# A two-layer hybrid decoder trunk on one core: 32x32 diagonal blocks inverted on VectorE, and one block level less on TensorE

## The reference, cut to what matters

```python
def chunked_gated_delta_rule(q, k, v, beta, g):
    ...
    lower = jnp.where(strict, jnp.einsum('bhncd,bhnsd->bhncs', k_beta, k) * decay, 0.0)
    eye = jnp.eye(GDN_CHUNK, dtype=lower.dtype)
    rhs = jnp.concatenate([v * beta[..., None], k_beta * jnp.exp(g)[..., None]], axis=-1)
    sol = lax.linalg.triangular_solve(lower + eye, rhs, left_side=True, lower=True, unit_diagonal=True)
    u = sol[..., :dv]
    w = sol[..., dv:]
    ...
    def step(state, xs):
        u_i, w_i, qd_i, intra_i, ks_i, cd_i = xs
        v_new = u_i - jnp.einsum('bhck,bhkv->bhcv', w_i, state)
        o_i = jnp.einsum('bhck,bhkv->bhcv', qd_i, state) + jnp.einsum('bhcs,bhsv->bhcv', intra_i, v_new)
        state = state * cd_i[..., None, None] + jnp.einsum('bhck,bhcv->bhkv', ks_i, v_new)
        return state, o_i
```

## Time and profile before

| | us |
|---|---|
| median of three executions | 2683.03 |
| the profiled execution | 2680.91 |
| its span, from the first to the last instruction | 2679.0 |
| TensorE busy (97%) | 2605.1 |
| VectorE busy (64%) | 1712.2 |
| ScalarE busy (44%) | 1176.7 |

### The profile page before, as it was taken

One profiled execution on the slowest core, in us unless ns is written; L12 is line 12 of the kernel. 1 busy time (PEld: TensorE's weight loads), 2 busy tenths in 40 slices (PEclk: granted clock), 3 DMA queues, 4 the chain that ended last, 5 costly groups with the idle time before them and its releaser, 6 DMA issues. The chain is left out here.

```text
span 2679.0 us, 35335 instructions
## 1 busy us (share of the span) xinstructions
PE 2605.1 (97%) x12554; PEld 2196.0 (82%) x12554; DVE 1712.2 (64%) x2296; ACT 1176.7 (44%) x1450; POOL 85.1 (3%) x89
## 2 busy tenths in 40 slices
PE   7998999999999999999999999999999999999997
PEld 7886888788887988788788888888788888888885
DVE  3356875787577766776666767666665645546556
ACT  1025354543555354635444444444454344453443
POOL 0000110011001000101000000000000000000000
PEclk9678999999999999999999999999999999999998
DMA  8676556764676558555688777876555665666655
GB/s 257 218 238 183 172 156 190 236 173 142 189 244 173 150 165 257 163 171 172 200 267 257 253 254 238 268 254 230 178 160 188 194 186 191 190 187 192 188 189 178
DMA packets 300997, 541.69 MB, mean 202 GB/s; under 512 B 39200, under 2 KB 44832, under 8 KB 299552
## 3 DMA queue, kind: packets, MB, share of 16 engines
q1 hardware_dynamic: 271568, 523.86, 62.8%
q10 hardware_dynamic: 29264, 15.68, 2.0%
HBM read 536.26 MB, written 3.21 MB: 201 GB/s over the span
## 5 line engine op out<-in xcount | busy, mean ns | idle before, releaser
L1038 DVE TENSOR_TENSOR w_lo<-raw,w_hi 128x1024 fp32r<-128x1024 f32 x803 | 986.0, 1228 | 700.0 <-ACT w_hi L606 658.0
L606 ACT ACTIVATE w_hi<-raw 128x1024 fp32r<-128x1024 f32 x803 | 847.5, 1060 | 1152.9 <-PE acc L1603 828.2
L1603 PE MATMUL acc<-w_hi,u_hi 128*128 128x512 f32 x2176 | 869.9, 400 | 8.3 <-DVE w_lo L1038 7.3
L1603 PE MATMUL acc<-w_hi,u_lo 128*128 128x512 f32 x2176 | 851.5, 391 | 0.0
L1603 PE MATMUL acc<-w_lo,u_hi 128*128 128x512 f32 x2176 | 850.8, 391 | 0.0
L1603 PEld LDWEIGHTS acc<-w_hi,u_hi 128*128 128x128 f32 x2176 | 411.6, 189 | 97.5 <-DVE w_lo L1038 14.5
L1603 PEld LDWEIGHTS acc<-w_hi,u_lo 128*128 128x128 f32 x2176 | 410.6, 189 | 87.9
L1603 PEld LDWEIGHTS acc<-w_lo,u_hi 128*128 128x128 f32 x2176 | 411.6, 189 | 81.3 <-issue 1.0
L1603 PE MATMUL acc<-w_hi,z_hi 128*128 128x512 f32 x1024 | 399.5, 390 | 0.1
L1603 PE MATMUL acc<-w_hi,z_lo 128*128 128x512 f32 x1024 | 398.6, 389 | 0.0
L1603 PE MATMUL acc<-w_lo,z_hi 128*128 128x512 f32 x1024 | 398.4, 389 | 0.0
(11 more groups left out here) (237 smaller groups left out, 1488.2 us busy)
## 6 DMA issues: line engine op xcount, KB each, us to landing
raw<-in_w_in SPq DMA_DIRECT2D x416, 512.0 KB, 4.5
raw<-in_w_ff SPq DMA_DIRECT2D x259, 512.0 KB, 4.3
raw<-in_w_ada SPq DMA_DIRECT2D x192, 512.0 KB, 4.6
raw<-in_w_branch_a SPq DMA_DIRECT2D x32, 512.0 KB, 5.2
raw<-in_w_branch_b SPq DMA_DIRECT2D x32, 512.0 KB, 4.9
raw<-in_w_branch_c SPq DMA_DIRECT2D x32, 512.0 KB, 4.9
raw<-in_w_o SPq DMA_DIRECT2D x32, 512.0 KB, 4.6
IT<-decay_d ACTq DMA_DIRECT2D x8, 512.0 KB, 6.6
```

Of the source, the lines that this page charges most:

```text
L606: a.activation(w_hi[:, u % PARTS, :, :], raw[:, rl % RAWS, :, :], ACT.Copy).then_inc(hi_ready.sem, 1)
L1038: v.tensor_tensor(w_lo[:, u % PARTS, :, :], raw[:, rl % RAWS, :, :], w_hi[:, u % PARTS, :, :], ALU.subtract).then_inc(lo_ready.sem, 1)
L1603: return t_.matmul(dst, lhsT, rhs, start=start, stop=stop)
```

## The change

VectorE inverts blocks of 32 x 32. There are 16 x 4 of them, and each is given to two partitions: both hold the whole block (blocks), and partition half n has the rows n, n + 2, ... of the inverse (inverse, eye). A step j works on j//2 + 1 rows and 31 - j columns. Level 4 is gone from LEVELS, with its matmuls, masks, additions and its transposes. The blocks are now in W_a, and beta is loaded for both halves. The inverse goes out in two DMAs whose pieces are single rows, and into TT in four. VectorE makes a unit after every second step (every third before). The chain starts at k-tile 101 (AT_W) instead of 86, everything of it up to FK is 12 k-tiles later than before from Y on, and the stages behind FK lie closer together. ScalarE takes FK out of its accumulator ahead of the chain.

```diff
-BK = 16
+BK = 32
 NBK = P // BK
-LEVELS = (4, 5)
+HALVES = 2
+ROWS = BK // HALVES
+LEVELS = (5,)
...
-AT_TOK, AT_BLOCKS, AT_MOD0, AT_INVERSE, AT_FQ = 67, 67, 70, 75, 82
-AT_W, AT_D = (86, 91), (88, 93)
-AT_Y, AT_Z, AT_X, AT_O = (95, 102), (96, 103), (98, 105), (99, 106)
-AT_KS, AT_FK = 100, 108
-AT_SCORES, AT_YB, AT_PROB, AT_YC, AT_CC, AT_CH = 114, 122, 132, 136, 139, 146
+AT_TOK, AT_BLOCKS, AT_MOD0, AT_INVERSE, AT_FQ = 67, 67, 70, 88, 82
+AT_W, AT_D = (101,), (103,)
+AT_Y, AT_Z, AT_X, AT_O = (107, 114), (108, 115), (110, 117), (111, 118)
+AT_KS, AT_FK = 112, 120
+AT_SCORES, AT_YB, AT_PROB, AT_YC, AT_CC, AT_CH = 125, 132, 140, 144, 146, 149
...
-        blocks = W_b[:, 0, 0:2, :].rearrange("p a (b c) -> p (a b) c", c=BK)
-        inverse = W_b[:, 0, 2:4, :].rearrange("p a (b c) -> p (a b) c", c=BK)
-        outer = W_b[:, 1, 0:2, :].rearrange("p a (b c) -> p (a b) c", c=BK)
+        blocks = W_a[:, :, :, :].rearrange("p a q (b c) -> p (a q b) c", c=BK)
+        inverse = W_b[:, 0, :, :].rearrange("p q (b c) -> p (q b) c", c=BK)
+        outer = W_b[:, 1, :, :].rearrange("p q (b c) -> p (q b) c", c=BK)
+        halves_at = [slice(n * P // HALVES, (n + 1) * P // HALVES) for n in range(HALVES)]
-        strict = sb("strict", [P, BK, BK])
-        eye = sb("eye", [P, BK, BK])
+        eye = sb("eye", [P, ROWS, BK])
...
-                at = (h * MT + t) * 2 * NBK
-                sp.dma_start(beta_b[at:at + 2 * NBK, :, :], src).then_inc(beta_in.sem, 16)
+                for n in range(HALVES):
+                    at = n * P // HALVES + (h * MT + t) * 2 * NBK
+                    sp.dma_start(beta_b[at:at + 2 * NBK, :, :], src).then_inc(beta_in.sem, 16)
...
-                act.dma_start(blocks, low_d[:, :, :, :].rearrange("q b s c -> (q b) s c")).then_inc(low_in.sem, 16)
+                for at in halves_at:
+                    act.dma_start(blocks[at], low_d[:, :, :, :].rearrange("q b s c -> (q b) s c")).then_inc(low_in.sem, 16)
...
-                to(AT_INVERSE)
-                wait("inv_made", 1)
-                act.dma_start(inverse_d[:, :, :, :].rearrange("q b s c -> (q b) s c"), inverse).then_inc(inv_out.sem, 16)
-                to(AT_INVERSE + 4)
-                act.wait_ge(inv_out.sem, inv_out.value(i, 16))
-                wait("tt_zero", 1)
-                for b in range(NBK):
-                    bs = slice(b * BK, (b + 1) * BK)
-                    act.dma_start(TT[bs, :, :, bs].rearrange("s h q c -> s (h q) c"),
-                                  inverse_d[:, b, :, :].rearrange("q s c -> s q c")).then_inc(inv_in.sem, 16)
                 to((J_FQ + 1) * KT)
...
+                to(AT_INVERSE)
+                wait("inv_made", 1)
+                for n, at in enumerate(halves_at):
+                    dst = inverse_d[:, :, :, :].rearrange("q b (s n) c -> n (q b) s c", n=HALVES)[n]
+                    act.dma_start(dst, inverse[at]).then_inc(inv_out.sem, 16)
+                to(AT_INVERSE + 4)
+                act.wait_ge(inv_out.sem, inv_out.value(i, 16 * HALVES))
+                wait("tt_zero", 1)
+                for b in range(NBK):
+                    bs = slice(b * BK, (b + 1) * BK)
+                    act.dma_start(TT[bs, :, :, bs].rearrange("s h q c -> s (h q) c"),
+                                  inverse_d[:, b, :, :].rearrange("q s c -> s q c")).then_inc(inv_in.sem, 16)
+                to((J_FK + 1) * KT + 1)
+                take_job(i, J_FK, stage[:, :, :])
...
-                        take_job(i, J_FK, stage[:, :, :])
...
-                tt(inverse, blocks, strict[:, :, :], ALU.mult)
-                o.after()
-                tt(inverse, inverse, eye[:, :, :], ALU.add)
-                for j in range(1, BK - 1):
-                    shape = [P, j, BK - 1 - j]
-                    o.after()
-                    tt(outer[:, 0:j, j + 1:BK], inverse[:, 0:j, j:j + 1].broadcast_to(shape),
+                copy(inverse, eye[:, :, :])
+                for j in range(BK - 1):
+                    n = j // HALVES + 1
+                    shape = [P, n, BK - 1 - j]
+                    o.after()
+                    tt(outer[:, 0:n, j + 1:BK], inverse[:, 0:n, j:j + 1].broadcast_to(shape),
                        blocks[:, j:j + 1, j + 1:BK].broadcast_to(shape), ALU.mult)
                     o.after()
-                    tt(inverse[:, 0:j, j + 1:BK], inverse[:, 0:j, j + 1:BK], outer[:, 0:j, j + 1:BK], ALU.add,
+                    tt(inverse[:, 0:n, j + 1:BK], inverse[:, 0:n, j + 1:BK], outer[:, 0:n, j + 1:BK], ALU.add,
                        *(("inv_made", 1) if j == BK - 2 else ()))
-                    if j % 3 == 0:
+                    if j % 2:
                         next_slot()
-                to(AT_MOD0 + 1)
-                mod_columns(0)
-                to(AT_FQ)
+                        if count[0] == AT_MOD0 + 1:
+                            mod_columns(0)
+                to(AT_W[0] - 2)
...
-                    if n == 0:
-                        o.after()
-                        turn_inverse(1)
```

More of the change, by code:

```diff
@@ L366, in layer_program @@
         low_out, inv_in = (signal(n, 16 * NBK) for n in ("low_out", "inv_in"))
-        low_in, inv_out = (signal(n, 16) for n in ("low_in", "inv_out"))
+        low_in, inv_out = (signal(n, 16 * HALVES) for n in ("low_in", "inv_out"))
         decay_in = signal("decay_in", 16 * MT)
@@ L530, in _ @@
                 o.do(g.memset(t[:, :], v))
-            o.do(g.memset(strict[:, :, :], 1.0))
             o.do(g.memset(eye[:, :, :], 0.0))
@@ L545, in _ @@
             keep(upper[:, :], [[1, P]], 0, -1)
-            keep(strict[:, :, :], [[-1, BK], [1, BK]], -1, 0)
-            keep(eye[:, :, :], [[-1, BK], [1, BK]], 0, 0, 1.0, ALU.not_equal)
+            for n, at in enumerate(halves_at):
+                keep(eye[at, :, :], [[-HALVES, ROWS], [1, BK]], -n, 0, 1.0, ALU.not_equal)
             keep(causal_big[:, :], [[-1, P]], 0, 1, BIG)
@@ L1313, in _ @@
                 to(AT_BLOCKS)
-                dve.wait_ge(low_in.sem, low_in.value(i, 16))
-                dve.wait_ge(beta_in.sem, 16 * KPC * MT)
+                dve.wait_ge(low_in.sem, low_in.value(i, 16 * HALVES))
+                dve.wait_ge(beta_in.sem, 16 * KPC * MT * HALVES)
                 tt(blocks, blocks, beta_b[:, bass.ds(i, 1), :].broadcast_to([P, BK, BK]), ALU.mult)
                 o.after()
-                tt(inverse, blocks, strict[:, :, :], ALU.mult)
-                o.after()
-                tt(inverse, inverse, eye[:, :, :], ALU.add)
-                for j in range(1, BK - 1):
-                    shape = [P, j, BK - 1 - j]
+                copy(inverse, eye[:, :, :])
+                for j in range(BK - 1):
+                    n = j // HALVES + 1
+                    shape = [P, n, BK - 1 - j]
                     o.after()
-                    tt(outer[:, 0:j, j + 1:BK], inverse[:, 0:j, j:j + 1].broadcast_to(shape),
+                    tt(outer[:, 0:n, j + 1:BK], inverse[:, 0:n, j:j + 1].broadcast_to(shape),
                        blocks[:, j:j + 1, j + 1:BK].broadcast_to(shape), ALU.mult)
                     o.after()
-                    tt(inverse[:, 0:j, j + 1:BK], inverse[:, 0:j, j + 1:BK], outer[:, 0:j, j + 1:BK], ALU.add,
+                    tt(inverse[:, 0:n, j + 1:BK], inverse[:, 0:n, j + 1:BK], outer[:, 0:n, j + 1:BK], ALU.add,
                        *(("inv_made", 1) if j == BK - 2 else ()))
-                    if j % 3 == 0:
+                    if j % 2:
                         next_slot()
-                to(AT_MOD0 + 1)
-                mod_columns(0)
-                to(AT_FQ)
+                        if count[0] == AT_MOD0 + 1:
+                            mod_columns(0)
+                to(AT_W[0] - 2)
                 def turn_inverse(n):
@@ L1854, in solve @@
                         if t == 0:
-                            wait("tt_made", KPC + h + 1)
+                            wait("tt_made", (len(LEVELS) - 1) * KPC + h + 1)
                             wait("vb_made", h + 1)
```

## The result

| | before | after |
|---|---|---|
| median of 11 executions each, us | 2680.82 (2677.92 to 2684.43) | 2690.39 (2685.78 to 2692.93) |
| the profiled execution, us | 2680.91 | 2686.23 |
| its span, us | 2679.0 | 2684.4 |
| mean granted clock in the span | 0.976 | 0.976 |
| last k-tile of the fourth pass starts, us | 1293.7 | 1299.2 |

The ratio is 1.0031, 95% interval 1.0022 to 1.0039: slower by 0.31%, 8.3 us of 2681. The whole difference of the spans, 5.4 us, is there when the loop ends; nothing behind it changed. The profiled execution is the second fastest of its kernel: 2685.8 us stands with a mean clock of 0.975, 2690.4 with 0.974, 2692.9 with 0.972. The part of the loss above the profiled one goes with a lower mean clock; where in those executions it fell, no trace shows.

What follows compares the result with a forecast made beforehand. TensorE, busy 2605.1 of 2679.0 us, was taken as the bound. -28.6 + 14.4 + 12.8 + 3.2 = +1.8 us, added to 2680.9 with 2.1 for the median, gave 2684.8 us; range for 8 in 10: 2672 to 2697.

Steps and rivals of the forecast that it cites:

- The level, -28.6: TensorE loses one block level, a group of W and one of D matmuls: -28.6 us in four passes.
- Late w_lo behind the inversion, +14.4: TensorE waits for w_lo from k-tile 78 to 86 behind VectorE's longer inversion: 3.6 us a pass, +14.4 us.
- The wait ahead of W, +12.8: At k-tile 101 W waits for T_a, from VectorE's transposes: 3.2 us a pass, +12.8 us.
- the walk: Engine orders traced forward: VectorE waits 1.2, 0.4, 1.5 and 0.5 us at four w_lo and starts the transposes at 617.0.
- Bounds: 0 to 4.6: Range given for the wait ahead of W at k-tile 101: 0 to 4.6 us.
- Waits for w_lo between k-tiles 88 and 100: Sign to look for, with ScalarE issuing DMAs before them, that ScalarE's short DMAs decide.
- rival 2: ScalarE's short DMAs between its k-tiles 88 and 92 make w_hi late and decide: +12.8, 2697.6 us; chance 0.13.
- D, +3.2: VectorE's masking of W gives D's last head its data 0.8 us late: +3.2 us.
- The stages behind FK, 0: Stages from FK on are pushed together without a new wait: 0, bounds 0 and 1 us a pass.
- Rival 3, the clock: TensorE's clock falls in the new wait ahead of W: 1.2 us a pass, +4.8, 2689.6 us; chance 0.25.
- Rival 1, that the ring keeps pace: Raw buffers land fast enough, W and D find their data, only the inversion's wait remains: -14.2, 2669 us; chance 0.20.
- The three waits of the forecast: Waits behind the inversion, ahead of W and at D; forecast wrong if they sum below 5 or above 9 us a pass.

Runs made afterwards that it cites:

- experiment 1: Kernel before without its first level (level 4) and the transposes behind it, rest of the order kept: 2652.86 us, ratio 0.9898.
- Experiment 4: Changed kernel with 17 of the 31 inversion steps left out, so the inverse is incomplete: 2659.24 us, ratio 0.9916.
- Experiment 2: Changed kernel with the second half's eight modulation pieces moved to units 53 to 60, behind the chain: 2664.07 us, ratio 0.9932.
- experiment 6: Changed kernel with the inverse written out in contiguous stretches, so its rows return in another order: 2688.48 us, ratio 1.0026.
- experiment 3: Changed kernel with GpSimd's products of vtok and beta held back until the inverse is made: 2685.01 us, ratio 1.0002.
- experiment 5: Changed kernel with W at k-tile 103 and D at 105, VectorE's transposes left in their old place: 2688.30 us, ratio 1.0026.
- experiment 9: Changed kernel with later chain, pieces behind it, denser units and GpSimd's products held back, plus ten extra mask instructions for the first head's W: 2661.65 us, 0.9938.

## Why the prediction came out as it did

**The level, -28.6: right.** 256 records fewer, and by itself worth 27 us (experiment 1).

**Late w_lo behind the inversion, +14.4: right in mechanism and place, 2.3 too dear.** The eighth w_lo was done at 595.34 where 595.3 was forecast; that they meet is partly luck, for the inversion began 0.8 us later (564.86 for 564.07) and took 30.5 us for 31.2. TensorE wanted it a little later than was worked out. The copy taken at 0.5 us took 0.43. The steps' rate (0.22 us for 56 elements) held. Experiment 4 shows that the steps are the cause.

**The wait ahead of W, +12.8: right in size (13.1), and in kind.** T_a began at 620.14 instead of 617.0: VectorE waited 1.5, 1.5 and 3.3 us for w_hi where the walk had 1.2, 0.4, 1.5 and 0.5. TensorE was later as well, by its own waits of 2.2 us and a pass that began 0.6 us later, so that the difference stayed; that two errors of 3 us cancel is luck. The cause given was the ring and the order of VectorE. Experiment 2 shows it: with the pieces away and ScalarE's DMAs in place the wait is gone. It also shows what the prediction didn't say. It had the four modulation pieces, left in their old place by the change, in its sum of VectorE's work, and not as what decides.

**The step that failed** is "Bounds: 0 to 4.6" of that part, which had room for late data only at W, and the walk under it, in which ScalarE issues the DMAs into TT without a wait for the landing of the inverse. "Waits for w_lo between k-tiles 88 and 100" were given to rival 2 alone. They came, 5.1 us in four passes. In the second pass ScalarE stood until the inverse had landed, 8.8 us after its second issue, and then issued for 2.57 us. The w_hi behind that began 3.1 us after its raw tile had landed (1.5, 1.9 and 2.5 us in the other passes); VectorE waited 3.3 us for it and TensorE 1.4. With longer pieces the inverse lands in 4.4 us for 7.0, and most of these waits are gone (experiment 6), without a gain.

**D, +3.2: right in kind, 0.9 too dear** (2.3). **The stages behind FK, 0: right**, no new wait.

**Rival 3, the clock, came true on top of the forecast.** In the changed kernel's profiled execution it took 1.9 us in one pass, and D didn't wait there, 0.75 us less: 1.2 net, as the rival had priced it. (Of the two readings behind that price, the 11 matmuls where full speed has 18 are 1.6 us lost in 4 and not 2.) Behind longer single waits a fall took up to 3.3 us (experiment 3), in experiment 5 up to 5.3. The median execution is 4.2 us longer than that one at a lower mean clock. That these 4.2 us are falls in other passes was not seen in a trace of theirs; experiment 3's profiled execution, where all four passes fell, is the nearest. The prediction asked only how long one wait is. By the Trainium skill's "TensorE: Matmul & The Clock Gate", section "What's actually happening", half rate is the default that activity releases. The traces agree in that half rate came behind idle time. How much idle time it takes they leave open: it came behind waits of 1.7 and 2.1 us in sum (experiments 5 and 9), and not behind three waits of 3.0 us with one of 0.75 after them.

**Rival 1, that the ring keeps pace**, was one line of constants away: 2669 us forecast for it, 2664 measured when the pieces were moved. **Rival 2** didn't decide, for ScalarE's issues were no longer than charged, and in experiment 2 the wait goes with all of them in place. But its sign was there, waits of TensorE behind ScalarE's DMAs, and in the trace they come from ScalarE: from its issues together with the landing that it waits for.

The forecast of +1.8 us became +9.6 between the medians (8.3 by the ratio). To +1.8 come 5.1 from waits that it had in no place, 1.9 and some 4.2 from the clock and 0.3 ahead of W, less 3.2 that two terms were too dear: 10.1.

The three waits of the forecast sum to 6.9 us a pass, between the 5 and 9 that it had set itself. The time of 2690.4 us lies in the range of 2672 to 2697, at the edge of the forecast's own 2680 to 2690; of the three outcomes "same" was held likeliest (0.45), and "slower" (0.35) came. The 2.1 us that were added for the median rest on three executions. Eleven have it at 2680.82, where the profiled one lies, so by these 2.1 us the absolute time was met by luck.

## What to carry to other kernels

When work moves to an engine that feeds the bound one just in time, list everything that shares its queue and its buffers in that stretch and move what has no due time out of it first; here that was worth 26 us and no instruction was saved. A saving ahead of a join is worth little while the other arm of the join is the late one (experiment 6). When one DMA must land before the same engine issues the next, count that landing as time in which the engine's other work stands still. Count waits of TensorE that lie close together as one risk to its clock: making them shorter in sum may give nothing (experiment 5).

## What the hardware showed that was not expected

- A wait of 1.5 us, with 0.2 to 1.4 us of wait some 6 us earlier, was followed by 7 to 10 us at half clock, 5.3 us lost in one pass; of the single waits ahead of W the two of 1.6 and 1.9 us were free of it, the eight of 2.5 to 3.1 had it three times, the six of 3.4 to 5.4 each time.
- A VectorE instruction of 0.19 us took 0.54 beside GpSimd's, one of 1.22 took 1.34 to 1.68.
- 1024 pieces of 128 bytes were issued in 0.65 us and landed, two such DMAs a pass, in 7.0 us in the median; with contiguous stretches it was 0.56 and 4.4.
